# Page turns written plainly and read with a large step by TensorE, gelu steps one step earlier

## The chip, the cores and the metric

The kernel runs on one core of one Trainium2 chip. The metric is the time of one launch on the device in microseconds (us). The profiled execution has a span, from its first to its last instruction, that is a little shorter than that time.

## The reference

One inference step of a one-layer decoder trunk for two groups of tokens: a prompt of 512 rows and a sample group of 8 sequences with 4 new tokens each. All of it is float32. What matters here is the attention of the sample group over a paged cache of keys and values (16 pages of 128 tokens for each of the 8 sequences, 8 heads of 64), and the gelu of two of the projections.

```python
proj = jnp.einsum('bsd,de->bse', rmsnorm(x, norm_g), w_in)     # 1024 -> 5632 columns
q, k, v, g_a, u, v_s, g_b, m_a, m_b = jnp.split(proj, SPLIT_POINTS, axis=-1)
u = jax.nn.gelu(u)
v_s = layernorm(jax.nn.gelu(v_s), ln_g, ln_b)
...
# sample group: blocks of 2 pages; per head and token the 3 best past blocks by q . mean(k)
k_full = cache_k[layer, page_table[:, :n_full * ppb]]
gate = jnp.einsum('bthd,bnhd->bhtn', q, k_mean)
_, sel = lax.top_k(gate, 3)
s_sel = jnp.einsum('bthd,bhtkd->bhtk', qf, k_sel) + bias
p = jax.nn.softmax(jnp.concatenate([s_sel, s_loc], axis=-1), axis=-1)
out = jnp.einsum('bhtk,bhtkd->bthd', p[..., :n_k_sel], v_sel) + ...
```

The outputs are the trunk's rows for both groups, the new keys and values, and the normalised v rows.

## The kernel before

Activations lie transposed in SBUF, features on the partitions and the 544 rows (512 prompt, 32 sample) along the free dimension. Each 128-column tile of the combined weight matrix is split into a high and a low part (`WH` on ScalarE, `WL` on GpSimd or VectorE), and TensorE makes each product from three matmuls of 272 columns in the rounded 32-bit type (line 583, later line 603 for the branch projections and line 922 for the output projection). These are most of TensorE's work.

After the first twelve tiles (q, k, v) the kernel runs an order written out by hand: `for t in range(STEPS)`, 144 steps, written separately for each engine's queue. In each step TensorE runs four pieces of the projection (`run(fill, 2)` twice) and between them the small pieces of the attention that are due at that step. Four steps go by for one weight tile. Each engine works its own list strictly in order, and semaphores tie them.

The sample group's scores need every page of keys with its features on the partitions. Step t, for t below 128, handles page t:

- SyncE (`load_k`, line 491) loads page t + 4 into `KRAW`, a ring of `KR` = 4 pages. It waits until VectorE has turned the page that held the slot. Its queue also carries the loads of the values (`load_v`, line 511, four pages at a time) and of the weights.
- VectorE (`page_turn`, line 1332) turns the page into `KT`, which holds `KB` = 8 pages: one stream transpose of 128x512 that turns blocks of 32x32. It waits for the load (`k_ld`) and until TensorE has read the pages that held the slot (`sc_pe`).
- TensorE (`page_scores(q)`, line 737), every fourth step, multiplies the queries `QW` (32 columns, stationary) with four pages. It makes 16 float32 products of 128 moving columns, in four rounds; the four products of a round write four 32-row groups of the bank and run side by side. Each product stands as two instructions in the trace, so a call is 32 instructions. The 128 moving columns are 32 tokens of each of four pages with the page as the inner index: column 4t + j is token t of page j. The order must be that one, since the values are loaded so (line 511) and the block sums read it so.

In the kernel before, `KT` is stored in that order. The transpose writes its elements 4 apart (16 bytes), and the matmul reads 128 elements in a row.

The gelu of a tile g (eight of them, 128x544) takes four operations: `gelu_square` and `gelu_tanh` on ScalarE (lines 1070 and 1074), `gelu_inner` and `gelu_outer` on VectorE (lines 1353 and 1358). They alternate, so each waits for the one before, through the buffer `TG`. They are due at steps 53 + 4g, 55 + 4g, 54 + 4g and 56 + 4g. Both operations on VectorE read two tensors in SBUF. On GpSimd, `split_lo` (line 1692) is due at steps divisible by 4, as soon as ScalarE has made `WH` in that step.

Of the kernel before, what the change touches and what calls it, by code (L numbers as in the profile page):

```python
# [15 lines left out]
P = 128  # L16
# [10 lines left out]
DA = NH * HD  # L27
# [15 lines left out]
KR = 4  # L43
VR_ = 4
KB = 8
# [195 lines left out]
def build(nc, x_p, x_s, cache_k, cache_v, page_table, rel_bias, norm_g, w_in, ln_g, ln_b, w_s, b_s, w_pa, w_pb,  # L241
          w_o, fin_g, cst, ini, sgc, y_p, y_s, k_p, v_p, k_s, v_s, sgu_s):
    with ExitStack() as ctx:
# [5 lines left out]
        def sb(name, shape, dt=F32):  # L249
            size = 4 * int(np.prod(shape[1:]))  # L250
            off = top[0]
            top[0] += (size + 31) // 32 * 32
            return at(name, shape, dt, off)

        def sem(name):
            return ctx.enter_context(nc.semaphore(name))
# [10 lines left out]
        WL = sb("WL", [P, 2, KC, P], F32R)  # L267
        kv_at = top[0]
        KRAW = sb("KRAW", [P, KR, DA])
        KT = sb("KT", [P, KB // 4, 16, 32, 4])  # L270
        v_at = top[0]
        VRAW = sb("VRAW", [P, VR_, DA])
        qk_at = top[0]
# [13 lines left out]
        QW = sb("QW", [P, 16, 32])  # L287
# [93 lines left out]
        SCB, OUT = [BK[4], BK[2]], BK[5]  # L381
# [28 lines left out]
        kt_ok, sc_pe, qr_pe, qr_ok, qw_ok, bw_ok = sem("kt_ok"), sem("sc_pe"), sem("qr_pe"), sem("qr_ok"), sem("qw_ok"), sem("bw_ok")  # L410
# [160 lines left out]
        def _(pe):  # L571
            mm = pe.matmul
# [50 lines left out]
            for x in range(4):  # L623
                q = slice(32 * x, 32 * x + 1)
                last = mm(BK[x][:, 0:DM // 4], ONE[q, :], GROW[q, :], start=True, stop=True, tile_position=(32 * x, 0))
# [66 lines left out]
            for n in range(2, N_QKV):  # L692
# [11 lines left out]
                if n == 5:  # L704

                    for x in range(4):
                        for b in range(4):
                            last = mm(BK[2][32 * b:32 * b + 32, x * P:(x + 1) * P], IDN[:, 32 * x:32 * x + 32], QT[:, :, SEQ:ROWS], start=True, stop=True)
                    last.then_inc(qr_pe, 1)
                if n == 9:  # L710
# [3 lines left out]
                    for b in range(NB):  # L714
                        for c in range(PAIRS):
                            last = mm(BK[3][32 * c:32 * c + 32, b * 32:(b + 1) * 32], QC[:, b, c, :], KTS[:, c, SEQ:ROWS], start=True, stop=True)
# [9 lines left out]
            def page_scores(q):  # L726

                b, x = q // 4, q % 4
                pe.wait_ge(kt_ok, 4 * q + 4)
                if x == 0:  # L730
                    pe.wait_ge(qw_ok, b + 1)

                    wait(pe, pt_ok, b - 1)
                for k in range(4):
                    for c in range(PAIRS):
                        f = 4 * c + k
                        last = mm(SCB[b % 2][32 * c:32 * c + 32, x * P:(x + 1) * P], QW[:, f, :], KT[:, q % 2, f].rearrange("p t j -> p (t j)"),  # L737
                                  start=(k == 0), stop=(k == 3))
                last.then_inc(sc_pe, 1)

# [228 lines left out]
        def _(act):  # L969
# [102 lines left out]
            def gelu_tanh(g):  # L1072
                act.wait_ge(ge_dve, 2 * g + 1)
                act.activation(TG[:], TG[:], ACT.Tanh, scale=GELU_C).then_inc(ge_act, 1)
# [49 lines left out]
            for t in range(STEPS):  # L1124
                n = N_QKV + t // 4
                if t % 4 == 0 and 4 <= t <= 128:
                    evict(n - 1, 1)
                    split_hi(n + 1)
                if t % 4 == 2 and t < 128:
                    evict(n, 0)  # L1130
                if t % 4 == 0 and t > 128:
                    split_hi(T_PB + 2 + (t - 132) // 4)
                if sample_at(t, scale_step) is not None:
                    scale_out(sample_at(t, scale_step))
                if block_at(t - 1) is not None:
                    prompt_exp(block_at(t - 1))
                if block_at(t - 3) is not None:
                    prompt_out(block_at(t - 3))
                if sample_at(t, exp_step) is not None:
                    exponentials(sample_at(t, exp_step))  # L1140
                if sample_at(t, probs_step) is not None:
                    probs_out(sample_at(t, probs_step))
                if t % 4 == 1 and 53 <= t < 85:
                    gelu_square((t - 53) // 4)
                if t % 4 == 3 and 55 <= t < 87:
                    gelu_tanh((t - 55) // 4)
                if t == 117:
                    act.wait_ge(yb_ok, 5)

                    act.wait_ge(pv_pe, 24)  # L1150
                    copy(YBH[:], G[:, GB:GB + 4, :]).then_inc(ybh_ok, 1)
                if 133 <= t < 133 + PAIRS:

                    c = t - 133
                    act.wait_ge(av_ev, len(BLOCKS))
                    act.wait_ge(pj, matmuls_before(T_PB))
                    copy(XH[:, c, 0:SEQ], G[:, GA + c, 0:SEQ]).then_inc(yah_ok, 1)
                if t == 141:
                    act.wait_ge(ot_ev, NB)
                    copy(XH[:, 0:4, SEQ:ROWS], G[:, GA:GA + 4, SEQ:ROWS]).then_inc(yah_ok, 1)  # L1160
# [41 lines left out]
        def _(dve):  # L1202
# [72 lines left out]
            for t in range(TD):  # L1275
                last = dve.tensor_copy(TB[:, t, t:t + 125:4].rearrange("p (g b h) -> p g b h", g=4, b=4),
                                       bass.AP(tab.tensor, tab.offset, [list(tab.ap[0]), [2, 4], [0, 4], [1, 2]]))
# [50 lines left out]
            def page_turn(i):  # L1328

                dve.wait_ge(k_ld[i % KR], 16 * (i // KR + 1))  # L1330
                wait(dve, sc_pe, (i - KB) // 4 + 1)
                dve.transpose(KT[:, i // 4 % 2, :, :, i % 4], KRAW[:, i % KR, :].rearrange("p (f d) -> p f d", f=16)).then_inc(kt_ok, 1)  # L1332

            def local_turn(b):
                dve.wait_ge(ex_ok, 2 * b + 2)
# [19 lines left out]
            def gelu_outer(g):  # L1355
                src = G[:, (GV if g < 4 else GU) + g % 4]
                dve.wait_ge(ge_act, 2 * g + 2)
                dve.scalar_tensor_tensor(out=src, in0=TG[:], scalar=1.0, in1=src, op0=ALU.add, op1=ALU.mult).then_inc(ge_dve, 1)
# [173 lines left out]
            for t in range(STEPS):  # L1532
                n = N_QKV + t // 4
                if t == 0:
                    rows_out(N_QKV - 1)
                if t < PAGES:
                    page_turn(t)
                if t % 4 == 0 and 4 <= t <= 128:
                    if T_GA <= n - 1 < T_GMA or T_GB <= n - 1 < T_GMB:
                        silu(n - 1, 1)  # L1540
                if t % 8 == 1 and 9 <= t < PAGES:
                    page_sums(t // 4 - 1)
                if t == PAGES:
                    page_sums(PAGES // 4 - 1)
                if block_at(t - 5) is not None:
                    prompt_gate(block_at(t - 5))
                if t % 4 == 2 and t < 128 and (T_GA <= n < T_GMA or T_GB <= n < T_GMB):
                    silu(n, 0)
                if block_at(t - 2) is not None:
                    prompt_norm(block_at(t - 2))  # L1550
                if sample_at(t, gate_step) is not None:
                    choose(sample_at(t, gate_step))
                if sample_at(t, probs_step) is not None:
                    local_turn(sample_at(t, probs_step))
                if sample_at(t - 1, sum_step) is not None:
                    sums_out(sample_at(t - 1, sum_step))
                if t % 4 == 0 and t > 128:
                    split_lo(T_PB + 2 + (t - 132) // 4)
                if sample_at(t - 1, out_step_of) is not None:
                    sample_out(sample_at(t - 1, out_step_of))  # L1560
                if t == 142:
                    dve.wait_ge(yah_ok, PAIRS + 1)
                    dve.tensor_tensor(XL[:, 0:4, SEQ:ROWS], G[:, GA:GA + 4, SEQ:ROWS], f32(XH[:, 0:4, SEQ:ROWS]), ALU.subtract).then_inc(yal_ok, 1)
                if block_at(t) is not None:
                    prompt_max(block_at(t))
                if t % 4 == 2 and 54 <= t < 86:
                    gelu_inner((t - 54) // 4)
                if t % 4 == 0 and 56 <= t < 88:
                    gelu_outer((t - 56) // 4)
                if t == 88:  # L1570
                    mask_mixing()
                if t == 89:
                    mask_sample_mixing()
                if t in (91, 93, 95, 97, 99):
                    norm_rows((t - 91) // 2)
                if t in (94, 96, 98, 100, 102):
                    norm_scale((t - 94) // 2)
                if t in (101, 103, 105, 107, 109):
                    spatial((t - 101) // 2)
                if 133 <= t < 133 + PAIRS:  # L1580
                    c = t - 133
                    dve.wait_ge(yah_ok, c + 1)
                    dve.tensor_tensor(XL[:, c, 0:SEQ], G[:, GA + c, 0:SEQ], f32(XH[:, c, 0:SEQ]), ALU.subtract).then_inc(yal_ok, 1)
                if t >= 129:
                    mixed_b(t - 129)
# [172 lines left out]
```

## Time and profile before

| | us |
|---|---|
| median of 3 runs | 554.54 (553.44 to 557.81) |
| the profiled execution, its time | 553.3 |
| the profiled execution, its span | 551.5 |
| TensorE matmul busy | 522.3 (95% of the span) |
| VectorE busy | 357.8 (65%) |
| ScalarE busy | 180.1 (33%) |
| GpSimd busy | 121.5 (22%) |
| mean granted TensorE clock | 0.983 of full speed |

Busy time is that of instructions that do work; waiting is not counted. Matmuls overlap, so the mean duration of one matmul is longer than the distance from one to the next; what a run of matmuls costs is read from the chain of work, which lists such runs with their length and count. TensorE's clock has two levels, and the granted clock is the mean over a stretch (1.0 is 2.4 GHz).

### The profile page before, as it was taken

What the parts mean: (1) busy time and instruction counts of PE and PEld (TensorE: products, weight loads), DVE (VectorE), ACT (ScalarE), POOL (GpSimd) and SP (SyncE); (2) the same over time, 40 slices, a digit from 0 to 9 for tenths busy, and PEclk for the clock granted to TensorE, in tenths of its full rate; (3) what the DMA queues carried; (4) which work ended last, traced back from release to release, by engine and by line L of the source; (5) the groups of instructions that cost most, each with busy time, mean ns of one, the idle gap of its engine ahead of it and who ended that gap; (6) DMA issues with size and microseconds to landing.
All of it is one profiled execution on the core that took longest, in us unless ns stands there. A gap on an engine that the chain in (4) does not pass through costs nothing.

```text
span 551.5 us, 13822 instructions
## 1 busy us (share of the span) xinstructions
PE 522.3 (95%) x5624; PEld 476.4 (86%) x5624; DVE 357.8 (65%) x678; ACT 180.1 (33%) x389; POOL 121.5 (22%) x108
## 2 busy tenths in 40 slices
PE   8999999998999999999899789979988999999994
PEld 6999999987899999998799689979988999998663
DVE  6624333688975876879886697998544454794524
ACT  5522222232442442353353232121151132333313
POOL 1201111231231231232213234622451300000002
PEclk9998999999999999999999899999997999999998
DMA  8645533378449678687498988867899692360004
GB/s 253 180 154 165 183 119 118 85 215 263 152 137 285 200 261 285 202 262 245 121 312 275 325 273 278 273 212 255 264 302 307 220 342 86 125 225 5 2 10 152
DMA packets 73561, 112.00 MB, mean 203 GB/s; under 512 B 5501, under 2 KB 35338, under 8 KB 73498
## 3 DMA queue, kind: packets, MB, share of 16 engines
q1 hardware_dynamic: 72122, 107.51, 60.2%
q0 software_dynamic: 1232, 3.36, 2.1%
q8 instruction: 44, 0.72, 0.6%
q10 hardware_dynamic: 144, 0.26, 0.1%
q14 instruction: 19, 0.16, 0.1%
HBM read 106.57 MB, written 4.53 MB: 201 GB/s over the span
## 4 chain that ended last, share of the span: by engine, by line
PE 70%; DVE 12%; SPq 7%; DMA 5%; issue 4%; ACT 0%; POOL 0%; POOLq 0%; DVEq 0%; ACTq 0%
PE BK L583 32%; PE BK L603 9%; PE BK L922 8%; DMA KRAW<-in_cache_k 5%; DVE KT L1332 5%; PE BK L737 4%; PE BK L751 3%; SPq L511 3%; PE BK L672 2%; PE BK L799 2%; PE BK L617 2%; PE BK L816 1%; PE BK L806 1%; SPq L491 1%; DVE NMX L1431 1%
## 5 line engine op out<-in xcount | busy, mean ns | idle before, releaser
L583 PE MATMUL BK<-XH,WH 128*128 128x272 f32 x672 | 203.8, 303 | 0.1
L583 PE MATMUL BK<-XL,WH 128*128 128x272 f32 x672 | 195.2, 290 | 0.0
L583 PE MATMUL BK<-XH,WL 128*128 128x272 f32 x672 | 195.1, 290 | 0.0
L1332 DVE STREAM_TRANSPOSE KT<-KRAW 128x512 f32<-128x512 f32 x128 | 137.8, 1118 | 36.9 <-DMA KRAW<-in_cache_k 36.7
L583 PEld LDWEIGHTS BK<-XH,WH 128*128 128x128 f32 x672 | 128.6, 191 | 11.2 <-issue 10.6
L583 PEld LDWEIGHTS BK<-XL,WH 128*128 128x128 f32 x672 | 128.5, 191 | 0.0
L583 PEld LDWEIGHTS BK<-XH,WL 128*128 128x128 f32 x672 | 128.1, 191 | 0.0
L1692 POOL TENSOR_TENSOR WL<-WRAW,WH 128x1024 fp32r<-128x1024 f32 x32 | 77.0, 2408 | 208.8 <-ACT WH L971 208.7
L971 ACT ACTIVATE WH<-WRAW 128x1024 fp32r<-128x1024 f32 x52 | 55.0, 1058 | 16.0 <-PE BK L603 16.0
L737 PE MATMUL BK<-KT,QW 128*32 128x128 f32 x1024 | 35.1, 278 | 13.9 <-DVE KT L1332 13.7
L1223 DVE TENSOR_TENSOR WL<-WRAW,WH 128x1024 fp32r<-128x1024 f32 x19 | 23.3, 1224 | 37.3 <-ACT WH L971 37.3
L737 PEld LDWEIGHTS BK<-KT,QW 128*32 128x32 f32 x1024 | 26.4, 110 | 19.4 <-DVE KT L1332 16.6
L1733 POOL TENSOR_TENSOR RSTD<-MS,NHALF 128x1 f32<-128x1 f32 (+1 forms) x5 | 3.6, 727 | 104.2 <-DVE MS L1621 104.2
L1427 DVE TENSOR_TENSOR BK<-BK,TPH 128x256 f32<-128x256 f32 (+1 forms) x32 | 10.8, 393 | 22.6 <-PE BK L799 22.6
L1062 ACT ACTIVATE G<-BK 128x272 f32<-128x272 f32 x16 | 6.4, 398 | 57.2 <-PE BK L583 57.1
L1104 ACT ACTIVATE APX<-BK,NMX 128x128 f32<-128x128 f32 (+3 forms) x32 | 16.5, 526 | 18.6 <-DVE NMX L1433 18.5
L971 ACT ACTIVATE APT<-BK 128x384 f32<-128x384 f32 (+1 forms) x24 | 11.3, 524 | 28.3 <-PE BK L806 28.3
L603 PE MATMUL BK<-YBH,WH 128*128 128x272 f32 x64 | 19.3, 301 | 0.0
L1046 ACT ACTIVATE TG<-BK 128x272 f32<-128x272 f32 x16 | 6.4, 398 | 39.1 <-PE BK L583 39.1
L922 PE MATMUL BK<-OH,MH 128*128 128x512 f32 x64 | 18.6, 397 | 0.0
L603 PE MATMUL BK<-YBL,WH 128*128 128x272 f32 x64 | 18.4, 288 | 0.0
L603 PE MATMUL BK<-XL,WH 128*128 128x272 f32 x64 | 18.4, 288 | 0.0
(207 smaller groups left out, 818.5 us busy)
## 6 DMA issues: line engine op xcount, KB each, us to landing
KRAW<-in_cache_k SPq DMA_DIRECT2D x128, 256.0 KB, 4.4
WRAW<-in_w_in SPq DMA_DIRECT2D x21, 1024.0 KB, 7.3
VRAW<-in_cache_v SPq DMA_DIRECT2D x56, 256.0 KB, 3.5
VQT<-in_cache_v SPq DMA_DIRECT2D x28, 256.0 KB, 3.9
VEX<-in_cache_v SPq DMA_DIRECT2D x24, 256.0 KB, 4.3
VGU<-in_cache_v SPq DMA_DIRECT2D x20, 256.0 KB, 3.8
WO<-in_w_o SPq DMA_DIRECT2D x4, 1024.0 KB, 6.4
XR<-in_x_prompt SPq DMA_DIRECT2D x4, 512.0 KB, 5.0
```

Of the source, the lines that this page charges most:

```text
L511: sp.dma_start(VP[place][j:P:4], cache_v[0, bass.ds(page, 1)].rearrange("a (b t) h d -> (a t) b (h d)", b=4)).then_inc(v_ld[place], 16)
L583: last = mm(BK[h][:, 0:HALF], w[:, n % 2, k, :], x[:, k, cols], start=(i == 0 and w is WH and x is XA), stop=(i == KC - 1 and w is WL))
L603: last = mm(bank[:, 0:HALF], w[:, n % 2, 4 * x + k, :], y[:, k, cols], start=(k == 0 and w is WH and y is XA), stop=(k == 3 and w is WL))
L617: mm(BK[bank][:, 0:256], VS[:, 0:P], VS[:, 0:256], start=True, stop=True)
L737: last = mm(SCB[b % 2][32 * c:32 * c + 32, x * P:(x + 1) * P], QW[:, f, :], KT[:, q % 2, f].rearrange("p t j -> p (t j)"), start=(k == 0), ...
L751: last = mm(OUT[32 * c:32 * c + 32, 0:P], PT[:, x, 32 * p:32 * p + 32], VP[place][:, p, c * P:(c + 1) * P], start=(x == 0 and p == 0), sto ...
L922: last = mm(OB[cb][r][:], x[:, k, r * P:(r + 1) * P], w[(n - T_WO) % 4][:, kk, :], start=(i == 0 and w is OH and x is MH), stop=(i == KC - ...
L971: return act.activation(o, i, ACT.Copy)
L1104: act.activation(APX[:, e, o:o + n], BK[6 + e][:, o:o + n], ACT.Exp, bias=NMX[:, 2 * x + e:2 * x + e + 1], scale=1.0 / UNIT, accum_out=PLS ...
L1223: dve.tensor_tensor(WL[:, n % 2], WRAW[:, n // 2 % 2, :, n % 2 * P:(n % 2 + 1) * P], f32(WH[:, n % 2]), ALU.subtract).then_inc(w_lo, 1)
L1332: dve.transpose(KT[:, i // 4 % 2, :, :, i % 4], KRAW[:, i % KR, :].rearrange("p (f d) -> p f d", f=16)).then_inc(kt_ok, 1)
L1692: pool.tensor_tensor(WL[:, n % 2], WRAW[:, n // 2 % 2, :, n % 2 * P:(n % 2 + 1) * P], f32(WH[:, n % 2]), ALU.subtract).then_inc(w_lo, 1)
```

## The change

Three edits. `KT` becomes a plain buffer of eight pages, each 128x512 as it comes from the transpose, and the transpose writes its elements one after the other. For the scores TensorE now reads a pattern: the page is the inner index with a step of 512 elements (2048 bytes), the token the outer one with a step of one element. The columns come in the same order as before. The buffer has the same size.

`gelu_tanh` moves from step 55 + 4g to step 54 + 4g, and `gelu_outer` from step 56 + 4g to step 55 + 4g. In its step each remains the last item of its engine's list but for those that are due at other steps.

```diff
-        KT = sb("KT", [P, KB // 4, 16, 32, 4])
+        KT = sb("KT", [P, KB, DA])
...
-                        last = mm(SCB[b % 2][32 * c:32 * c + 32, x * P:(x + 1) * P], QW[:, f, :], KT[:, q % 2, f].rearrange("p t j -> p (t j)"),
+                        last = mm(SCB[b % 2][32 * c:32 * c + 32, x * P:(x + 1) * P], QW[:, f, :], KT[:, 4 * (q % 2):4 * (q % 2) + 4, 32 * f:32 * f + 32].rearrange("p j t -> p t j"),
                                   start=(k == 0), stop=(k == 3))
...
-                if t % 4 == 3 and 55 <= t < 87:
-                    gelu_tanh((t - 55) // 4)
+                if t % 4 == 2 and 54 <= t < 86:
+                    gelu_tanh((t - 54) // 4)
...
-                dve.transpose(KT[:, i // 4 % 2, :, :, i % 4], KRAW[:, i % KR, :].rearrange("p (f d) -> p f d", f=16)).then_inc(kt_ok, 1)
+                dve.transpose(KT[:, i % KB, :], KRAW[:, i % KR, :]).then_inc(kt_ok, 1)
...
-                if t % 4 == 0 and 56 <= t < 88:
-                    gelu_outer((t - 56) // 4)
+                if t % 4 == 3 and 55 <= t < 87:
+                    gelu_outer((t - 55) // 4)
```

## Rows read from the trace of the kernel before

**Rows 1.** The page, busy time by engine: us, share, instructions.

```profile
PE 522.3 (95%) x5624; PEld 476.4 (86%) x5624; DVE 357.8 (65%) x678; ACT 180.1 (33%) x389; POOL 121.5 (22%) x108
```

**Rows 2.** Busy time by stretch: stretch, its length, busy by engine, PEclk, DMA share, GB/s.

```profile
100.00:450.00 350.00, 331.16 (x4178) 305.65 (x4176) 264.17 (x507) 115.53 (x278) 102.82 (x79) 0.99 0.76 245
130.00:150.00 20.00, 17.98 (x173) 15.91 (x172) 17.10 (x36) 5.44 (x12) 5.68 (x6) 1.00 0.55 172
240.00:330.00 90.00, 80.87 (x1037) 75.24 (x1036) 75.73 (x128) 35.24 (x84) 24.09 (x17) 0.98 0.79 254
350.00:370.00 20.00, 16.31 (x240) 15.15 (x240) 19.41 (x38) 4.88 (x11) 9.14 (x10) 1.00 0.70 220
400.00:440.00 40.00, 36.06 (x462) 34.28 (x461) 18.49 (x36) 10.64 (x21) 14.36 (x5) 0.91 0.83 276
...
310.00:315.00 5.00, 4.47 (x71) 4.09 (x72) 3.16 (x4) 0.66 (x1) 3.86 (x5) 0.66 0.86 309
415.00:420.00 5.00, 4.58 (x74) 4.20 (x75) 2.82 (x5) 0.00 (x0) 1.04 (x1) 0.67 0.95 321
420.00:425.00 5.00, 5.00 (x29) 5.00 (x29) 3.12 (x5) 0.40 (x1) 0.00 (x0) 0.64 0.85 279
```

**Rows 3.** Waits of the whole span, SyncE's queue last: total us, times, longest us.

```profile
DVE KT L1332 <- DMA KRAW<-in_cache_k: 36.7, 16, 6.0
...
ACT TG L1070 <- DVE G L1358: 9.9, 5, 3.1
...
PE BK L737 <- DVE KT L1332: 13.7, 8, 3.8
...
SPq L490 <- DVE KT L1332: 102.3, 52, 15.0
```

**Rows 4.** Groups of instructions on VectorE, by form: busy us, mean ns of one.

```profile
L1337 DVE STREAM_TRANSPOSE PLT<-SCL 128x32 f32<-128x32 f32 x8 | 1.5, 186 | 0.0
L1431 DVE TENSOR_REDUCE NMX<-BK 128x1 f32<-128x128 f32 x8 | 2.0, 286 | 0.1
L1284 DVE COPY RS<-BK 128x512 f32<-128x512 f32 x4 | 2.8, 689 | 2.9 <-PE BK L652 2.9
```

**Rows 5.** Single lines of VectorE: duration ns minimum/median/maximum, first and last start.

```profile
L1332 DVE STREAM_TRANSPOSE KT<-KRAW x128: 1043/1102/1255, 105.3 to 434.7; 128x512 f32<-128x512 f32 x128
L1321 DVE TENSOR_REDUCE B<-BW x1: 382/382/382, 42.0 to 42.0; 128x32 f32<-128x128 f32 x1
L1353 DVE SCALAR_TENSOR_TENSOR TG<-TG,G x8: 679/702/718, 242.7 to 320.7; 128x544 f32<-128x544 f32 x8
L1358 DVE SCALAR_TENSOR_TENSOR G<-TG,G x8: 693/2608/2910, 246.4 to 323.7; 128x544 f32<-128x544 f32 x8
```

**Rows 6.** Timeline of VectorE and GpSimd, a gelu_outer each at 246 and 298 us.

```profile
246.10 2.37 POOL L1692 TENSOR_TENSOR WL<-WRAW,WH 128x1024 fp32r<-128x1024 f32 x1 [8.44 <-ACT WH L971]
246.45 2.61 DVE L1358 SCALAR_TENSOR_TENSOR G<-TG,G 128x544 f32<-128x544 f32 x1
298.33 0.69 DVE L1358 SCALAR_TENSOR_TENSOR G<-TG,G 128x544 f32<-128x544 f32 x1
299.28 2.38 POOL L1692 TENSOR_TENSOR WL<-WRAW,WH 128x1024 fp32r<-128x1024 f32 x1 [6.53 <-ACT WH L971]
```

**Rows 7.** Chain of work in order of time: start us, length us, what.

```profile
174.91 1.51 PE BK L583 x12
181.70 1.01 PE BK L737 x32
182.71 0.87 PE BK L751 x32
493.24 27.60 PE BK L922 x120
```

## The prediction

> **What bounds the kernel now.** I read the busy times first: TensorE's matmuls are busy for 522.3 of 551.5 us, so the kernel is bound by TensorE, and VectorE with 357.8 us is second [rows 1]. Next I read the same numbers by stretch. From 100 to 450 us, the steps in which pages are handled, TensorE lacks 350 - 331.16 = 18.84 us. Nearly all of it lies in four stretches: 2.0 us at 130 to 150, 9.1 at 240 to 330, 3.7 at 350 to 370 and 3.9 at 400 to 440 [rows 2]. In the second and third VectorE is busy for 75.7 of 90 and 19.4 of 20 us: there VectorE sets the pace. In the fourth it is busy for only 18.5 of 40 us while the DMA engines are at 0.83: there the transfers do. After two of the stalls the granted clock falls to 0.64 to 0.67, a mixture of its two levels, for 5 and 10 us. What that costs is the busy time times what is missing from 1: 4.47 x 0.34 + 4.58 x 0.33 + 5.00 x 0.36 = 4.8 us.
>
> The waits say by what: TensorE's scores wait 13.7 us for turned pages. VectorE waits 36.7 us for raw pages, while SyncE, which issues their loads, waits 102.3 us for VectorE to free the slots [rows 3]. It is a ring: a late turn makes a late load, and this a late turn. So all that can be won is 18.8 + 4.8 = 23.6 us. A cost on TensorE itself has no such limit, since nothing hides it.
>
> **Part 1, VectorE's write.** 128 transposes of 128x512 take 1043 ns at least, 1102 at the median [rows 5]. Their cost with a plain write isn't in the trace. The same operation with 128x32 and a plain write takes 186 ns [rows 4], and a plain copy with 512 elements 689 ns [rows 4]. From 186 ns on, 480 more elements at the copy's pace (at most 689/512 = 1.35 ns, and 1.05 ns if its fixed part is 150) give 690 to 830 ns; I take 690. Per element the present ones cost (1043 - 186)/480 = 1.79 ns at their fastest, where a plain pattern costs 1.05. So a turn gets 0.41 us cheaper and VectorE is relieved of 128 x 0.41 = 53 us. The other end is nothing at all, if the large form of the transpose is slow for another reason than its write.
>
> **Part 2, TensorE's read.** This is the part that decides. A call of the scores has 32 instructions of 128 columns and takes 1.01 us, the values with as many 0.87 us [rows 7]. Four run side by side, so eight follow one another, 0.87/8 = 109 ns each or 0.85 ns for each column. After the change each of these columns lies 2048 bytes from the next. No row shows such a read by TensorE. The ends are as follows.
>
> The low end is nothing. The 272-column matmuls take 1.51/12 = 126 ns, 0.46 ns for each column [rows 7]. TensorE's read of plain 32-bit data is thus shown to be nearly twice as fast as the float32 scores need it. If a large step halves the pace that is possible, the scores don't feel it. I put no gain below nothing, since the columns and rounds stay the same.
>
> The high end comes from VectorE. Its reduce at line 1321 reads 128 elements in SBUF with an inner step of 128 bytes and takes 382 ns. A reduce of 128 elements with a step of one takes 286 ns [rows 4, 5]. The difference is 0.75 ns for each element, on top of 1.04, so 1.79 ns. That is the 1.79 ns of the transposes' write. Two different operations, one in its read and one in its write, have the same pace, and it isn't a whole number of VectorE's own steps of 1.04 ns. This speaks for a limit in time and not for one in steps of the engine: one small piece of memory every 1.79 ns. TensorE's matmuls speak for it as well. Between 272 and 512 columns (27.60/120 = 230 ns each [rows 7]) a column costs (230 - 126)/240 = 0.43 ns, four of them 1.74 ns, about the same again. At 1.79 ns instead of 0.85 for each column an instruction takes 229 ns instead of 109, and a call 8 x 0.120 = 0.96 us longer. With 32 calls that is +30.7 us. All of it lies on TensorE. Much more than that would come of the four columns groups' reads taking turns; but side by side in the values they already fetch twice as many columns in the same time as the 272-column matmuls (4/0.85 = 4.7 against 2.2 for each ns), so each has its own way in, and I leave this out of the sum. I take the high end, since two rows of VectorE and the slope on TensorE agree with one figure, and the low end needs a limit counted in the engine's own steps, which 1.79 against 1.04 doesn't show.
>
> The Trainium skill has a rule that speaks against this change: "SBUF — State Buffer", section "Door 1: The DMA port swizzle", says that SBUF is read in lines of 16 bytes and that full bandwidth takes at least two hits on a line; "Advanced Engine Details and Errata", section "Memory Cachelines", says the same. By it the transpose's write, with one hit for each line, leaves the penalty, and TensorE's read, four hits before, enters it. The trace agrees for VectorE (1.79 against about 1.05 ns). The pages give no price for TensorE; by the rule alone the sum would lie anywhere between the two ends above.
>
> **Part 3, the gelu steps.** `gelu_outer` takes 2608 ns at the median and 693 at least, while `gelu_inner` of the same size takes 702 [rows 5]. The timeline shows why. At 246.45 it starts while GpSimd's split, started at 246.10, runs until 248.47, and it ends 0.6 us after that. At 298.33, before GpSimd's next, it takes 0.69 [rows 6]. One step sooner it stands before the step in which GpSimd starts its split. That takes (2187 - 700) x 8 = 12 us from VectorE, with 2187 ns as the mean of the eight, and they all lie in the stretch from 240 to 325 us, where VectorE sets the pace. ScalarE's `gelu_square` no longer waits 9.9 us for it [rows 3].
>
> The Trainium skill's "SBUF — State Buffer", section "Who interferes with whom", says that a VectorE operation with two SBUF inputs and a GpSimd operation that reads SBUF block each other for the whole instruction; the trace agrees with it (2608 against 693 ns).
>
> What it adds: `gelu_tanh` stands in step 54 + 4g directly behind `gelu_inner` and waits for it. Behind it in ScalarE's queue stand the exponentials of the prompt blocks at steps 59 and 75. VectorE's maximum of these blocks is made before `gelu_inner`, so they start some 0.7 + 0.7 us later than they could. TensorE turns them two steps later, so I count nothing; without that cover it would be 2 x 1.4 us. `gelu_outer` has only one page turn (0.69 us) between itself and `gelu_inner`, as long as the tanh takes; it may wait some tenths of a us, eight times, hardly 2 us of the 12. Neither moved step issues a DMA, and SyncE's list stays as it is.
>
> **The sum.** VectorE is relieved by 53 + 12 us in 350, so it no longer sets TensorE's pace: pages are turned sooner and SyncE issues the loads sooner. What stays late: at 130 to 150 us the softmax of the prompt blocks goes back and forth between VectorE and ScalarE, and at 400 to 440 us the transfers, where three more loads of values fall due. With calls that take 0.96 us longer TensorE asks for less in the same time, so I leave 2 of the 18.8 us of idle time and 0.6 of the 4.8 of the clock. Made against the profiled time: 553.3 + 30.7 - 16.8 - 4.2 = 563.0 us; the profiled run lies 1.2 us below the median, and I forecast 564.
>
> **The rivals.**
> A. TensorE reads the pages as fast as before (the limit lies in the engine's own steps, so that it halves 0.46 ns at most to 0.92, within a tenth of the 0.85 of the scores). For it: float32 uses only half the pace. Against it: the 1.79 ns. Then TensorE's work is as before and the stalls go, less 4 us of idle and 1.5 of clock, as the transfers are asked for sooner: 553.3 - 14.8 - 3.3 = 535 us, faster. With 0.92 for 0.85 it would be 32 x 8 x 128 x 0.07 ns = 2 us more. It decides from the price of a call: the break-even is (16.8 + 4.2)/32 = 0.66 us for each call, 1.6 times what it is.
> B. The read is slowed, but partly: the step is felt in each line, yet the four groups hide some of it. At half of 0.96 us it would be 553.3 + 15.4 - 20 = 549 us.
> C. The change doesn't do what it says: the transpose stays at 1.10 us, since its size and not its write makes it slow. Then only the 12 us at 240 to 325 are won, of which perhaps 8 reach TensorE. With the dear read: 553.3 + 30.7 - 8 and some stalls hidden by it, 571 us. With the free read 545.
>
> **Chances.** Forecast 0.50, A 0.35, B 0.09, C 0.06 (both forms together). The forecast's own range is 558 to 570: a page's read may cost 0.8 to 1.1 us more for each call, and 0 to 5 us of idle time may stay. The range that leaves out no more than 2 in 10 has to reach A, so 532 to 570. A measurement of this kernel can tell about 1% from no change (5.5 us). Faster than that: A and a third of B, 0.38. Within: most of B and the low edge of the forecast, 0.13. Slower: 0.49.
>
> **What would show it.** In the profile after, line 1332 should be near 0.69 us each and `gelu_outer` near 0.7. A call of the scores should stand in the chain with some 1.9 us for 32 instructions, and TensorE's busy time should come to about 550 us. The scores' waits for turned pages should be nearly gone, and the clock without the falls at 310 and 415 us. If the 32 instructions still take 1.0 us, part 2 is wrong and A holds. If the transposes stay at 1.1 us, part 1 is wrong. If both are as I say and the stalls remain, the transfers and not VectorE were behind them.

## The result and the profile after

| | us |
|---|---|
| before, median | 556.17 (553.44 to 561.16, 4 runs) |
| after, median | 572.44 (571.64 to 578.56, 4 runs) |
| after, the profiled execution | 578.56, span 576.8 |

The ratio after to before is 1.030, with an interval of 1.020 to 1.039: 3% slower. The sign is that of the forecast, and TensorE's dear read is there. The size isn't that of the forecast: 564 us were forecast, and 572.4 lies above the range of 532 to 570. The profiled execution is the slowest of the runs of this kernel; the others lie between 571.3 and 573.1.

The page of the kernel after, the busy line and two groups:

```profile
PE 556.3 (96%) x5624; PEld 506.1 (88%) x5624; DVE 307.2 (53%) x678; ACT 184.8 (32%) x389; POOL 121.2 (21%) x108
...
L1332 DVE STREAM_TRANSPOSE KT<-KRAW 128x512 f32<-128x512 f32 x128 | 88.3, 707 | 53.9 <-DMA KRAW<-in_cache_k 53.7
L737 PE MATMUL BK<-KT,QW 128*32 128x128 f32 x1024 | 73.8, 430 | 10.0 <-DVE KT L1332 10.0
```

The page of the kernel before has for the scores:

```profile
L737 PE MATMUL BK<-KT,QW 128*32 128x128 f32 x1024 | 35.1, 278 | 13.9 <-DVE KT L1332 13.7
```

TensorE is busy with the scores for 73.8 us where it was 35.1, so 38.7 us more, or 1.21 for each of the 32 calls (2.31 against 1.10). In the chain of work of the kernel after a call looks like this (start, length, what; some of its 32 instructions overlap the next ones and are counted there):

```profile
187.27 2.15 PE BK L737 x28
189.42 0.99 PE BK L751 x29
```

The values behind it take 0.99 us where they took 0.87 [rows 7]. VectorE's two lines (duration minimum/median/maximum, first and last start) answer to [rows 5]:

```profile
L1332 DVE STREAM_TRANSPOSE KT<-KRAW x128: 667/704/884, 105.6 to 459.2; 128x512 f32<-128x512 f32 x128
L1358 DVE SCALAR_TENSOR_TENSOR G<-TG,G x8: 724/776/2428, 257.8 to 339.5; 128x544 f32<-128x544 f32 x8
```

A turn costs 0.70 us where it was 1.10, and `gelu_outer` 0.78 at the median where it was 2.61. VectorE's busy time fell by 50.6 us [rows 1]. The stretch in which pages are handled, in the view by stretch:

```profile
100.00:460.00 360.00, 349.96 (x3969) 320.93 (x3968) 204.76 (x480) 115.34 (x265) 101.02 (x79) 1.00 0.71 228
```

TensorE lacks 10.0 us here, against 18.84 [rows 2]. The span can be put together from this. It grew by 25.3 us. The scores bring +38.7 and TensorE's idle time in the whole span fell by 8.7 (551.5 - 522.3 = 29.2, 576.8 - 556.3 = 20.5). TensorE's whole busy time grew by 34.0 us, 4.7 less than the scores' own. Two things lie in these 4.7 us. The falls of the clock cost 4.8 us before [rows 2]; in the kernel after one is left, and by the same reckoning it costs 1.4 us (TensorE is busy for 2.63 us from 325 to 330 us at a granted clock of 0.87, and for 5.00 us from 330 to 335 at 0.79: 2.63 x 0.13 + 5.00 x 0.21). That is 3.4 us less. The remaining 1.3 us are most likely time in which the first products of the values already run beside the last ones of the scores, which the whole counts once. I did not measure it.

### The profile page after: what moved, and what is told of

It is laid out like the page before. It is cut to its first block, busy times and chain, and to the rows that moved or that the text cites. A ratio compares the mean times of both kernels' runs of the same rounds, so it can differ in the third digit from the quotient of the medians.

```text
span 576.8 us, 13822 instructions
## 1 busy us (share of the span) xinstructions
PE 556.3 (96%) x5624; PEld 506.1 (88%) x5624; DVE 307.2 (53%) x678; ACT 184.8 (32%) x389; POOL 121.2 (21%) x108
## 4 chain that ended last, share of the span: by engine, by line
PE 79%; SPq 7%; DMA 5%; DVE 4%; issue 2%; POOL 1%; ACT 1%; POOLq 0%; DVEq 0%; ACTq 0%
PE BK L583 35%; PE BK L737 9%; PE BK L603 8%; PE BK L922 8%; DMA KRAW<-in_cache_k 5%; PE BK L751 4%; SPq L511 3%; PE BK L672 2%; PE BK L799 2%; PE BK L617 2%; PE BK L816 2%; PE BK L806 1%; SPq L491 1%; DVE KT L1332 1%; SPq L495 1%
## 5 line engine op out<-in xcount | busy, mean ns | idle before, releaser
L1692 POOL TENSOR_TENSOR WL<-WRAW,WH 128x1024 fp32r<-128x1024 f32 x32 | 78.2, 2445 | 231.9 <-ACT WH L971 231.8
L1332 DVE STREAM_TRANSPOSE KT<-KRAW 128x512 f32<-128x512 f32 x128 | 88.3, 707 | 53.9 <-DMA KRAW<-in_cache_k 53.7
L737 PE MATMUL BK<-KT,QW 128*32 128x128 f32 x1024 | 73.8, 430 | 10.0 <-DVE KT L1332 10.0
L737 PEld LDWEIGHTS BK<-KT,QW 128*32 128x32 f32 x1024 | 52.0, 125 | 20.1 <-DVE KT L1332 11.8
L971 ACT ACTIVATE WH<-WRAW 128x1024 fp32r<-128x1024 f32 x52 | 59.9, 1152 | 16.0 <-PE BK L603 16.0
L971 ACT ACTIVATE APT<-BK 128x384 f32<-128x384 f32 (+1 forms) x24 | 11.3, 524 | 30.7 <-PE BK L806 30.7
```

The costliest lines, as they stand in the source:

```text
L971: return act.activation(o, i, ACT.Copy)
L1332: dve.transpose(KT[:, i % KB, :], KRAW[:, i % KR, :]).then_inc(kt_ok, 1)
L1692: pool.tensor_tensor(WL[:, n % 2], WRAW[:, n // 2 % 2, :, n % 2 * P:(n % 2 + 1) * P], f32(WH[:, n % 2]), ALU.subtract).then_inc(w_lo, 1)
```

## The experiments

The step, group and skewed kernels (step2, step4, step16, one_of_four, two_of_four, skewed) were executed once each, so for these only the busy times of their one trace are compared and no ratio is given.

In what follows "idle" is what TensorE lacks between 100 and 460 us of the profiled execution (before 18.8, after 10.0), and "a call" is the busy time of line 737 divided by 32 (before 1.10, after 2.31). Ratios are to the kernel before on the same chip. Line numbers may differ by a few in kernels with lines added.

### Which part of the change costs

**kt_only**: the changed kernel with the gelu steps of before.

```diff
-                if t % 4 == 2 and 54 <= t < 86:
-                    gelu_tanh((t - 54) // 4)
+                if t % 4 == 3 and 55 <= t < 87:
+                    gelu_tanh((t - 55) // 4)
...
-                if t % 4 == 3 and 55 <= t < 87:
-                    gelu_outer((t - 55) // 4)
+                if t % 4 == 0 and 56 <= t < 88:
+                    gelu_outer((t - 56) // 4)
```

> The buffer, the write and the read of the change, with the gelu steps where they were. My theory: the loss is the read of the scores alone, so a call stays at 2.15 to 2.2 us and the 128 turns at 0.70 us, and gelu_outer goes back to 2.2 us in the mean. The 12 us of VectorE that this costs are mostly hidden, since TensorE is now much slower: 573 us, 0 to 3 us above the changed kernel. Rival, the gelu steps do the harm (ScalarE held behind the tanh): this kernel is some 15 us faster than the changed one, near the kernel before.

574.22 us, ratio 1.033 (1.026 to 1.040). A call 2.29 us. The whole loss is there without the gelu steps. One part of the expectation fell: `gelu_outer` did not go back to a mean of 2.2 us. Its median stayed at 0.77, and it takes over 2 us in 2 of 8 cases (3.87 and 2.22), where before it did in 6. So with cheap turns it seldom meets GpSimd's split even at its old place.

**gelu_only**: the reverse of that diff, in the kernel of before.

> The gelu steps of the change in the kernel of before. My theory: gelu_outer falls from a mean of 2.19 us to under 1 us, VectorE gets 8 to 12 us in the stretch of 240 to 330 us where it sets the pace, and 3 to 8 us of TensorE's 9.1 us of idle time there go: 549 us (546 to 553), ratio 0.985 to 0.995. Rival, the order on ScalarE costs as much as it wins: ratio 1.00 or above.

558.03 us, ratio 1.002 (0.998 to 1.006): nothing, the rival's number. The line itself did what it should (one case of eight above 1 us):

```profile
L1358 DVE SCALAR_TENSOR_TENSOR G<-TG,G x8: 697/716/2598, 245.6 to 325.6; 128x544 f32<-128x544 f32 x8
```

But idle is 24.2 us, and the scores wait 17.1 us for turned pages instead of 13.7. VectorE's relief of the stretch from 240 to 330 us (busy 67.1 us there, before 75.7) did not reach TensorE.

**plain_read**: the changed kernel with TensorE reading the four pages one after the other, 32 tokens in a row each.

```diff
-  KT[:, 4 * (q % 2):4 * (q % 2) + 4, 32 * f:32 * f + 32].rearrange("p j t -> p t j"),
+  KT[:, 4 * (q % 2):4 * (q % 2) + 4, 32 * f:32 * f + 32],
```

> The changed kernel, but TensorE reads the four pages one after the other, 32 tokens in a row each, so each 16 bytes give four columns. The columns come in another order than the later steps take them to have. My theory: the price lies in the step of the read, so a call falls back to 1.0 us and, with the turns at 0.70 us, the time is what the free read would have given: 535 us (532 to 541). Rival, the price lies in something else that changed with the buffer (a pattern of two dimensions, or VectorE's write beside TensorE's read): calls stay above 1.5 us and the time above 550 us.

549.13 us, ratio 0.983 (0.973 to 0.993). A call 1.13 us (36.3/32). So the price lies in the step of the read, and a pattern of two dimensions costs next to nothing. But the time is 549 and not 535: without the dear read only some 8 us are won, and idle is 14.9 us. VectorE now waits 58.1 us for raw pages, where it waited 36.7 [rows 3].

### What TensorE pays for a read with a step

**step2** and **step4** take every second or every fourth element of the four turned pages (steps of 8 and 16 bytes), **step16** every sixteenth (64 bytes). The columns are other ones than the reference needs.

```diff
+  # step4; step2 has 112 * f, 255 and :2, step16 has f, 2033 and :16
-  KT[:, 4 * (q % 2):4 * (q % 2) + 4, 32 * f:32 * f + 32].rearrange("p j t -> p t j"),
+  KT[:, 4 * (q % 2):4 * (q % 2) + 4, :].rearrange("p j e -> p (j e)")[:, 96 * f:96 * f + 509:4],
```

> The changed kernel, but TensorE's 128 columns are every second element (a step of 8 bytes), so two of them lie in each 16 bytes. The columns aren't those of the reference. My theory, one piece of 16 bytes every 1.9 ns for each group: 0.97 ns for each column against the 0.85 that float32 needs, so a call takes 1.1 to 1.2 us. Rival, any step is dear: 2.15 us. Rival, the limit is a large distance, not the number of pieces: 1.0 us.

> As step2 with every fourth element (a step of 16 bytes): one column in each 16 bytes, as near together as such columns can be. The columns aren't those of the reference. My theory: the same price as with 2048 bytes, 2.15 us for a call. Rival, the distance makes the price (2048 bytes end in the same part of the memory): clearly less, near 1.0 us.

> As step4 with every sixteenth element (a step of 64 bytes). The columns aren't those of the reference. A step of 16 bytes gave 1.94 us for a call, one of 2048 bytes 2.06 to 2.20. If the price of one column in each 16 bytes is the same for every distance, 1.94. If a longer step has its own price, between 1.94 and 2.2; this tells whether the 0.2 us more of the change come of the distance.

The groups of these kernels, first step2, then step4:

```profile
L737 PE MATMUL BK<-KT,QW 128*32 128x128 f32 x1024 | 36.0, 279 | 13.0 <-DVE KT L1332 13.0
```

```profile
L737 PE MATMUL BK<-KT,QW 128*32 128x128 f32 x1024 | 64.6, 406 | 7.1 <-DVE KT L1332 7.1
```

| step of the read | busy, 32 calls | a call | more than before |
|---|---|---|---|
| 4 bytes (before) | 35.1 | 1.10 | |
| 8 bytes (step2) | 36.0 | 1.13 | 0.03 |
| 16 bytes (step4) | 64.6 | 2.02 | 0.92 |
| 64 bytes (step16) | 61.8 | 1.93 | 0.83 |
| 2176 and 1920 bytes (skewed, below) | 66.9 | 2.09 | 0.99 |
| 2048 bytes (after) | 73.8 | 2.31 | 1.21 |

The jump lies between 8 and 16 bytes. Two columns in each 16 bytes are free (plain_read too has 1.13), one column in each costs 0.83 to 0.92 us for a call. That is nearly the 0.96 of the prediction, at its distance of 16 to 128 bytes. Step2 came as expected (1.1 to 1.2), and so did step16 (1.94 to 2.2). Step4 was expected to cost what 2048 bytes cost, and a call is 0.29 us cheaper (2.02 against 2.31). With the Trainium skill ("SBUF — State Buffer", section "Door 1: The DMA port swizzle") the trace agrees: two hits on a line of 16 bytes keep the bandwidth, one doesn't.

**one_of_four** and **two_of_four**: of the four products that run side by side only the first one or two read with the large step, the others read runs of 32. The columns of those come in another order.

```diff
-  .rearrange("p j t -> p t j"),
+  .rearrange("p j t -> p t j" if c == 0 else "p j t -> p j t"),   # two_of_four: if c < 2
```

> The changed kernel, but of the four products that run side by side only the first reads with the large step; the other three read four runs of 32 elements. Their columns come in another order. My theory: each of the four groups has its own way to the memory and is slowed by itself, so the first group alone takes 8 instructions of about 250 ns and a call stays at 2.0 to 2.2 us. Rival, the four share one supply that gives so many pieces of memory in a time: then the price goes with the number of groups that step, and a call takes about 1.0 + 1.15/4 = 1.3 us.

> As one_of_four, with two of the four products of a round reading with the large step. Measured so far: none 1.01 us for a call, one 1.57, all four 2.06 to 2.20. If each group alone had its own limit, two would be as dear as one (1.57). If they shared one supply, the price would go in equal steps, 1.01, 1.30, 1.6, 1.9, 2.2, which one_of_four has already missed. My theory now is both: one stream alone has its own limit of some 1.4 ns for each column, and on top of it streams that step get in each other's way, so two give 1.7 to 1.9 us.

In the chain a call of one_of_four stood at 1.57 us, and I built the expectation of two_of_four on it. That was a misreading. The timeline of one_of_four shows it (start, length, what):

```profile
182.66 1.74 PE L737 MATMUL BK<-KT,QW 128*32 128x128 f32 x31
184.00 0.42 PE L751 MATMUL BK<-VRAW,PT 128*32 128x128 f32 x6
184.23 0.40 PE L737 MATMUL BK<-KT,QW 128*32 128x128 f32 x1
```

The last instruction of the scores ends at 184.63, 1.97 us after the first began, while the other three groups are done and have gone on to the values at 184.00. The busy times are 62.5 us for one group, 68.7 for two and 73.8 for four: a call takes 1.95, 2.15 and 2.31 us. So the first stream pays nearly everything (+0.85) and the others only a little (+0.2, then +0.16). A supply that all share would have given 1.3 us for one. With two, 2.15 us came where 1.7 to 1.9 were expected. Each group has a limit of its own, (1.95 - 1.10)/8 = 0.11 us more for each instruction of 128 columns, and on top of it they hinder each other a little. One stream with a step of 2048 bytes makes the call about as long (1.95) as four with a step of 64 do (1.93), so what is dearer at 2048 bytes comes with the second to fourth stream.

**skewed**: the step between the columns of a token is 544 elements (480 for the last blocks) in place of 512. The columns are other ones.

```diff
+  kt = KT[:, 4 * (q % 2), 32 * f:32 * f + 32]
+  kt = bass.AP(kt.tensor, kt.offset, [list(kt.ap[0]), [1, 32], [544 if f < 13 else 480, 4]])
```

> The changed kernel, with a step between the four columns of a token of 544 or 480 elements (2176 or 1920 bytes) in place of 512 (2048 bytes). The columns aren't those of the reference. TensorE is busy with a call for 2.29 us in the changed kernel, for 2.02 with a step of 16 bytes and for 1.93 with one of 64. If the 0.3 us more come of the four groups meeting in the same part of the memory because 2048 is a round distance, a call falls to 1.9 to 2.0 us here. If they come of the distance as such, or of the two-dimensional pattern, it stays at 2.2 to 2.3.

2.09 us for a call, between the two expected values: three fifths of what 2048 bytes cost beyond 64 bytes (0.22 of 0.38) are gone with a distance as long but not round. That the groups meet in the same part of the memory fits this and the small price of the second and fourth stream. It isn't settled: the skewed read also spreads its columns over other blocks, and 0.16 us above 64 bytes remain.

### Where the stalls come from

**page_major** has the plain write and the plain read, and gives the reference's results. The bank of the scores holds its columns page by page, and VectorE puts them in order where it reads the bank anyway:

```diff
-  sc = SCB[b % 2][:, 2 * x * P:(2 * x + 2) * P].rearrange("p (k n) -> p n k", n=4)
-  summed = dve.tensor_reduce(R[:, 4 * x:4 * x + 4], sc, AX.X, ALU.add)
+  sc = SCB[b % 2][:, 2 * x * P:(2 * x + 2) * P].rearrange("p (k n t) -> p n k t", n=4, t=32)
+  summed = dve.tensor_reduce(R[:, 4 * x:4 * x + 4], sc, AX.XY, ALU.add)
...
-  dve.tensor_tensor(SC[:].rearrange("p (x k n) -> p x k n", x=2, n=4), SCB[b % 2][:].rearrange("p (x k n) -> p x k n", x=2, n=4),
-                    bass.AP(sel.tensor, sel.offset, [list(sel.ap[0]), [4, 2], [0, 64], [1, 4]]), ALU.add)
+  for x in range(2):
+      half_of = slice(2 * x * P, 2 * (x + 1) * P)
+      dve.tensor_tensor(SC[:, half_of].rearrange("p (k t n) -> p k t n", k=2, n=4), SCB[b % 2][:, half_of].rearrange("p (k n t) -> p k t n", k=2, n=4),
+                        bass.AP(sel.tensor, sel.offset + 4 * x, [list(sel.ap[0]), [0, 2], [0, 32], [1, 4]]), ALU.add)
```

> The plain write and the plain read both, with the order of the columns put right by VectorE where it reads the bank: the two sums and the maximum over tokens take patterns, and the addition that fills SC is made in two halves whose pattern reads the bank with a step of 32 elements. My theory: the bank is read by VectorE at full pace with a step (383 ns for 256 elements with a step of 16 bytes before), so it costs 8 x 0.2 us on VectorE and nothing on TensorE: 536 us (532 to 542), 3.5% faster than before. Rival, VectorE's reads of the bank become dear (reduces and additions at 1.8 ns for each element, some 8 x 2 us, on the chain from the scores to the probabilities): 545 us or more.

548.28 us, ratio 0.985 (0.979 to 0.991). The reordering is cheap, as expected. The sum, and the addition in two halves, take (the first line has minimum/median/maximum, the second busy time and mean):

```profile
L1367 DVE TENSOR_REDUCE R<-BK x16: 382/385/425, 120.6 to 433.4; 128x4 f32<-128x256 f32 x16
L1401 DVE TENSOR_TENSOR SC<-BK,SEL 128x256 f32<-128x256 f32 x16 | 5.9, 413 | 0.0
```

The sum took 374 ns at the median before. The halves take 413 ns each, so 2 x 413 in place of one of 682, which is 1.2 us in the whole kernel. The time, though, is 12 us above the expectation, like that of plain_read. It lies where the rival put it (545 or more), but not for the rival's reason. The profiled execution (550.1 us) even has an idle of 18.9 us, as much as the kernel before, and that of page_major_old_gelu below (542.6 us) 13.1. The gain of 1.5% stands in the medians; which stall it comes from isn't shown. The view by stretch of page_major shows TensorE standing while VectorE isn't full and the DMA engines first have little to do and then too much:

```profile
260.00:270.00 10.00, 10.00 (x128) 9.13 (x128) 7.79 (x19) 4.19 (x9) 4.00 (x5) 1.00 0.23 63
280.00:290.00 10.00, 7.59 (x111) 7.17 (x109) 5.97 (x10) 3.33 (x8) 2.37 (x1) 1.00 0.95 324
300.00:310.00 10.00, 5.22 (x76) 5.01 (x77) 4.89 (x8) 2.54 (x4) 3.09 (x4) 0.89 1.05 374
```

Between them stands this in SyncE's queue (timeline of page_major):

```profile
267.80 3.00 SPq L511 DMA_DIRECT2D VQT<-in_cache_v  x4
271.87 2.98 SPq L511 DMA_DIRECT2D VRAW<-in_cache_v  x4
275.04 0.97 SPq L491 DMA_DIRECT2D KRAW<-in_cache_k  x2
```

For 7.2 us SyncE issues two loads of values and no page of keys. VectorE then waits for a raw page, in this kernel 60.6 us in all. The kernel after has the same at 286 to 294 us, and a page issued soon after, at 295.42, takes 9.42 us to land in the crowd (by the chain of work; the timeline of the kernel after):

```profile
285.90 3.00 SPq L511 DMA_DIRECT2D VQT<-in_cache_v  x4
289.97 3.61 SPq L511 DMA_DIRECT2D VRAW<-in_cache_v  x4
293.77 0.97 SPq L491 DMA_DIRECT2D KRAW<-in_cache_k  x2
```

**page_major_old_gelu** is page_major with the first diff of this section.

> page_major with the gelu steps of the kernel before. In the kernel before the earlier gelu steps gave nothing (ratio 1.002), though they took 8 us from VectorE. My theory: VectorE isn't what TensorE waits for once the turns are cheap, so the gelu steps give nothing here either: 548 us, within 0.5% of page_major (0.985). Rival, they are worth their 8 us now: 553 us or more.

547.38 us, ratio 0.985 (0.980 to 0.990), the same as page_major. The gelu steps give nothing there either.

**page_major_spread**: extra loads later.

```diff
-  first = {1: 8, 11: 64, 25: 113, 26: 115, 27: 117}
+  first = {1: 8, 11: 64, 25: 113, 26: 118, 27: 122}
...
+                if t == 78:    # SGC and WSR, in place of 72
+                if t == 85:    # LNG and LNB, in place of 72
```

> page_major, and SyncE's extra loads are spread: the mixing weights from step 72 to 78, the two layer-norm rows from 72 to 85, and of the three extra loads of values those at steps 115 and 117 go to 118 and 122. In page_major TensorE still stands for some 14 us of its 19 while VectorE is free and waits for raw pages, and the DMA engines are at 0.95 to 1.05 at 280 to 310 and 400 to 430 us. My theory: the pages' loads are held up in these bursts, so 3 to 6 us of that go: 544 us (540 to 547). Rival, the loads are late because SyncE stands in its queue for TensorE and not because of the bursts: no change, 548 us.

544.84 us, ratio 0.979 (0.974 to 0.984). The intervals of the two overlap, so this alone is not shown to gain.

**page_major_queue**: page_major_spread, and the four pages of a load of values are issued in four successive steps, one behind each page of keys. Only the load that is due four steps before its use stays together.

The diff shows only the place where they are called.

```diff
-                    if load_step(q) == t:
-                        load_v(q)
+                    if q == 11:
+                        if t == 64:
+                            load_v(q)
+                    elif 0 <= t - load_step(q) - (q == 12) < 4:
+                        load_v(q, (t - load_step(q) - (q == 12),))
```

> page_major_spread, and SyncE issues the four pages of values of a load in four successive steps and not all in one (but those for step 64). In page_major the value loads hold SyncE for 3.9 us at a time (0.86 for the page numbers, four issues of 0.6 to 0.8), twice in a row at 268 to 275 us, and VectorE then waits up to 3.9 us for a raw page. My theory: SyncE's queue is what now holds the pages up, so 3 to 8 us of the remaining 14 us of TensorE's idle time go: 540 us (536 to 543), ratio 0.965 to 0.975 to the kernel before. Rival, the transfers themselves are the limit in these stretches (DMA share 0.95 to 1.05): no change from page_major_spread, 0.979.

536.22 us (532.67 to 536.76), ratio 0.962 (0.957 to 0.966), by 3.8% faster than the kernel before. Idle is 8.4 us. In its timeline the pages of keys now stand between the values (here four of the lines between 270 and 276 us):

```profile
270.77 0.72 SPq L499 DMA_DIRECT2D VRAW<-in_cache_v  x1
271.69 0.45 SPq L491 DMA_DIRECT2D KRAW<-in_cache_k  x1
...
272.81 0.61 SPq L499 DMA_DIRECT2D VRAW<-in_cache_v  x1
273.61 0.55 SPq L491 DMA_DIRECT2D KRAW<-in_cache_k  x1
```

The edit frees the queue and it also spaces out the transfers of the values. The two weren't tried apart. That the pages of keys were held up at their issue, and not by the crowd behind it, is my reading of the 7.2 us and isn't shown.

**queue_only** has the two queue edits in the kernel of before, **after_queue** in the changed kernel.

> The kernel of before with the loads spread as in page_major_queue (value loads one page in each step, the extra loads later), the buffer and gelu steps as before. It tells what the cheap turns are worth. My theory: VectorE and SyncE's queue held TensorE one after the other, so neither alone gives the whole: VectorE is as loaded as before at 240 to 330 and 350 to 370 us, and this kernel gets some 5 us, ratio 0.985 to 0.995. Rival, the queue was all of it: as page_major_queue, 0.962.

> The changed kernel with the same spread loads. TensorE's added work of some 37 us hid part of the stalls. With the loads spread there is nothing left to hide in, so it should gain less than page_major did (12 us): 566 us (562 to 569), ratio 1.012 to 1.022; its distance to page_major_queue (536 us) is then the whole price of the read, 30 to 37 us. Rival, the stalls were as large in the changed kernel: 560 us.

| | loads as before | loads spread |
|---|---|---|
| dear turns, plain read (before) | 1.000 | 0.981 (0.975 to 0.988), 549.4 us |
| cheap turns, plain read (page_major) | 0.985, 548.3 us | 0.962, 536.2 us |
| cheap turns, large step (after) | 1.030, 572.4 us | 1.017 (1.012 to 1.022), 566.7 us |

Queue_only gained more than was expected of it (0.981 against 0.985 to 0.995); after_queue came as expected. Both causes are real and nearly add up: 0.981 x 0.985 = 0.966 against 0.962. TensorE's scores wait for turned pages for 13.7 us before, 8.5 in queue_only and 6.8 in page_major_queue. One of these waits is mended by neither. It lies where the layer norm of the v rows takes some 14 us of VectorE besides the turns. It is 3.1 us before and in queue_only, and 2.5 in page_major and page_major_queue. In page_major_queue the same work lies some 12 us earlier (350 to 370 us of queue_only, then 340 to 360 of page_major_queue):

```profile
350.00:370.00 20.00, 16.33 (x209) 14.81 (x198) 18.84 (x36) 3.23 (x8) 8.57 (x9) 0.83 0.72 224
```

```profile
340.00:360.00 20.00, 16.99 (x198) 15.68 (x190) 18.35 (x38) 4.41 (x13) 8.12 (x10) 0.91 0.82 264
```

In after_queue idle is down to 2.6 us: with the dear read and the spread loads there is hardly anything left to win. Its distance to page_major_queue is 30.5 us (measured on two chips), the price of the read with VectorE's reordering as the only other difference: 37.5 us of busy time for the scores (72.8 against 35.3), less the 5.8 us of idle time that the slower kernel doesn't have and what the groups that are done early give to their followers.

## Why the prediction was wrong

**What bounds the kernel.** TensorE, right. That VectorE sets the pace in the second and third stretch was right for the third (350 to 370 us), but it is the layer norm that fills VectorE there, and turns cheaper by 0.4 us took only 0.6 of the 3.1 us of waiting. For the second it was at most half right: there the loads of values held the pages up as well. The row was before me as the 102.3 us that SyncE waits for VectorE [rows 3], and I read the ring in one direction only. I did not look at what stands in SyncE's queue between two pages.

**Part 1.** Right: a turn was forecast at 0.69 us and took 0.70. VectorE was relieved by 50.6 us instead of 65. By line, the turns gave back 49.5 of 53 (137.8 against 88.3) and `gelu_outer` 8.0 of 12 (17.5 against 9.5), since it still met GpSimd twice. That the whole fell by 6.9 us less than these two is because overlapping lines are counted once in it, and they overlap less after (by 20 us against 30).

**Part 2.** The mechanism was right and the term too small: +0.96 us for a call and +30.7 in all were forecast, +1.21 and +38.7 came. The 0.96 was taken from VectorE's reads and writes with steps of 16 and 128 bytes, and with steps of 16 and 64 bytes TensorE pays about that (0.92 and 0.83). The error was to carry the price of all four groups over to 2048 bytes and to leave their hindering each other there out of the sum. I had argued that each group has its own way in; one_of_four bears that out, but four with a step of 2048 bytes still cost 0.36 us more than one. The term is 8.0 us too small, and the range's upper end, set by "0.8 to 1.1 us more for each call", was too low for it. One of the three supports of the 0.96 was none: the 0.43 ns for each further column of a matmul are about one period of TensorE's clock (1/2.4 GHz = 0.42 ns), so that four of them come near 1.79 ns says nothing of the memory.

**Part 3.** Of the 12 us on VectorE 8.0 came here and 9.9 in gelu_only (8 x (2.187 - 0.947)), but they were worth nothing on TensorE: 1.002 alone, no difference in page_major or kt_only.

**The sum's last term, the recovered stalls.** This is the other step that failed. VectorE "no longer sets TensorE's pace: pages are turned sooner and SyncE issues the loads sooner", and this was to take away 16.8 of 18.8 us of idle time. In the profiled execution 8.8 went. With cheap turns VectorE stood waiting for raw pages instead, 53.7 us here and 60.6 in page_major where it had been 36.7. Of the 10.0 us that remain 7.4 went when the loads were spread (after_queue). Of the 4.2 us of the clock 3.4 came. So against the profiled time the sum misses by 8.0 us in the read and by 8.0 in the stalls, and the small rest is in the clock and the overlap. The median lies 6 us below the profiled execution, and the forecast for it was 8.4 us too low. The read's part of that is the same 8 us, if a call costs there what it costs in the two profiled executions (2.31 here, 2.29 in kt_only); how much TensorE stood in such an execution isn't known. The prediction named the transfers as the cause if the stalls stayed with cheap turns. It was the loads, their issue or the crowd that they make, and the runs don't part the two.

**Rival A** did not hold: the read is slowed. Its price of 535 us was wrong too, for the same reason as the last term. With a cheap read the kernel took 549 us (plain_read) and 548 (page_major); 536 us it is only with the loads spread as well. Rival B's and C's conditions did not arise.

## What to carry to other kernels

Moving a penalty for a large step from an engine that waits to one that never does is a loss even where its total gets smaller: here VectorE gave back 50 us, which alone were worth 8 us of time (page_major), and the scores took 39, of which some 30 counted even beside the fastest kernel (after_queue against page_major_queue). Look first for a place that can reorder for nearly nothing, here VectorE's reads of the bank (1.2 us). When a chain of waits goes round a ring (load, turn, free slot, load), read every queue on it before putting the stall down to its busiest engine, and ask what else that queue issues between two items of the ring.

## What the runs showed of the hardware

- TensorE's read of float32 moving columns costs nothing more at a step of 8 bytes (1.13 us for a call, as in plain_read), and nearly double at 16 (2.02). VectorE's transpose takes 1.10 us with a step of 16 bytes in its write and 0.70 with none; no run has 8 bytes there. The four column groups pay it side by side (1.95 us with one of them, 2.31 with all four), so that one bad stream in four is nearly as long as four bad ones. It leaves the others free for what follows (the values start at 184.00 us, the last product of the scores ends at 184.63).
- A step of 2048 bytes costs more than one of 64 (2.31 against 1.93), and part of that goes with a step that isn't round (2.09).
- VectorE's reduces read the bank with the innermost run of 32 elements, or with a step of 16 bytes, at the same pace (385 and 374 ns at the median for 256 elements).
- `gelu_outer` overlaps GpSimd's split, and then takes over 2 us, in 6 of 8 cases before. Cheap turns alone bring that to 2 of 8 (kt_only, the median is 0.77 us) and the earlier place alone to 1 of 8 (gelu_only, 0.72), so either of the two is enough for most of them.
